# Two transformer blocks in one program: the first product of the feed-forward and of the perceptron is made in turned form, with weights stationary

## What is computed

```python
def swiglu(h, w_ffn_in, w_ffn_out):                 # first block, layers l = 0, 1
    gu = h @ w_ffn_in                               # 256x1024 @ 1024x5632
    g, u = gu[..., :FFN_HIDDEN], gu[..., FFN_HIDDEN:]
    return (jax.nn.silu(g) * u) @ w_ffn_out         # 256x2816 @ 2816x1024

def sq_relu_mlp(x, w_in, w_out):                    # second block, layers i = 0, 1
    return jnp.square(jax.nn.relu(x @ w_in)) @ w_out   # 1024x4096, 4096x1024

for l in range(DEPTH):
    mod = (cond @ ada_w[l] + ada_b[l])[:, None, :]  # 1024x6144 per layer
    ...
    h = rmsnorm(x, norm2_g[l]) * (1 + sc2) + sh2
    x = x + g2 * swiglu(h, w_ffn_in[l], w_ffn_out[l])
```

## Time and profile before

| | us |
|---|---|
| median of 3 runs (1517.55 to 1520.44) | 1519.28 |
| the profiled execution's own time | 1520.99 |
| its span, first to last instruction | 1519.2 |
| PE busy | 1477.3 (97%) |
| POOL busy | 1217.4 (80%) |
| DVE busy | 714.1 (47%) |
| ACT busy | 711.8 (47%) |
| DMA moved | 313.79 MB, 207 GB/s |
| PE's granted clock, mean | 0.993 |

### The profile page before, as it was taken

The page is one execution under the profiler, slowest core; times in us unless marked ns, Lnnn a source line. Parts: engine busy times, 40 slices in busy tenths (PEclk is TensorE's granted clock), DMA queues, the critical chain, the costliest instruction groups (busy, mean ns, idle before and its releaser), DMA issues.

```text
span 1519.2 us, 20262 instructions
## 1 busy us (share of the span) xinstructions
PE 1477.3 (97%) x7242; PEld 1223.3 (81%) x7242; DVE 714.1 (47%) x1398; ACT 711.8 (47%) x1074; POOL 1217.4 (80%) x984
## 2 busy tenths in 40 slices
PE   7999999999999999999999999999999999999997
PEld 4897788788888987888788887878888887788886
DVE  7576755665643758755532104265331043644212
ACT  3335554544444444554544444365554345455432
POOL 4789997698797986548799897907998978289994
PEclk9999999999999999999999999999999999999999
DMA  9995555699876985425676675624665656166553
GB/s 357 323 379 162 183 155 164 203 356 298 288 267 182 385 293 163 132 93 181 208 245 196 192 221 158 211 74 140 193 191 185 208 171 213 45 175 194 185 184 107
DMA packets 168238, 313.79 MB, mean 207 GB/s; under 512 B 11061, under 2 KB 36041, under 8 KB 168137
## 3 DMA queue, kind: packets, MB, share of 16 engines
q1 hardware_dynamic: 166384, 311.15, 63.9%
q10 hardware_dynamic: 1754, 1.35, 0.3%
HBM read 311.39 MB, written 1.06 MB: 206 GB/s over the span
## 4 chain that ended last, share of the span: by engine, by line
PE 82%; POOL 7%; DVE 5%; ACT 2%; DMA 2%; issue 1%; SPq 0%; DVEq 0%; ACTq 0%; POOLq 0%
PE bank L693 72%; POOL lo_units L656 6%; PE bank L2076 2%; PE bank L838 1%; DMA raw_units<-in_w_in 1%; PE bank L859 1%; POOL mod_rows L633 1%; PE bank L827 1%; PE bank L826 1%; PE bank L825 1%; ACT hi_units L1112 1%; PE bank L877 1%; DMA mod_rows<-in_ada_w 1%; DVE bank L1434 1%; POOL mod_rows L637 1%
## 5 line engine op out<-in xcount | busy, mean ns | idle before, releaser
L656 POOL TENSOR_TENSOR lo_units<-raw_units,hi_units 128x512 fp32r<-128x512 f32 (+3 forms) x944 | 1167.7, 1272 | 264.8 <-ACT hi_units L1112 263.6
L693 PE MATMUL bank<-hi_units,turned 128*128 128x512 f32 (+2 forms) x2688 | 834.2, 385 | 7.7 <-POOL lo_units L656 6.0
L1112 ACT ACTIVATE hi_units<-raw_units 128x1024 fp32r<-128x1024 f32 (+3 forms) x478 | 485.5, 1018 | 539.4 <-PE bank L693 433.2
L693 PEld LDWEIGHTS bank<-hi_units,turned 128*128 128x128 f32 x2688 | 502.5, 189 | 103.4 <-POOL lo_units L656 9.0
L693 PE MATMUL bank<-lo_units,turned 128*128 128x512 f32 (+3 forms) x1344 | 512.2, 381 | 0.0
L693 PE MATMUL bank<-hi_units,turned_wide 128*128 128x512 f32 x992 | 312.1, 392 | 1.9 <-DVE turned_wide L1482 1.9
L693 PEld LDWEIGHTS bank<-lo_units,turned 128*128 128x128 f32 x1344 | 254.3, 189 | 41.8 <-issue 0.2
L693 PEld LDWEIGHTS bank<-hi_units,turned_wide 128*128 128x128 f32 x992 | 186.9, 188 | 41.2 <-DVE turned_wide L1482 2.2
L693 PE MATMUL bank<-lo_units,turned_wide 128*128 128x512 f32 x496 | 193.8, 391 | 0.0
L1434 DVE SCALAR_TENSOR_TENSOR bank<-ada_units,small,bank 128x512 f32<-128x512 f32 x144 | 108.8, 756 | 51.9 <-DMA ada_units<-in_ada_w 47.7
L693 PEld LDWEIGHTS bank<-lo_units,turned_wide 128*128 128x128 f32 x496 | 93.6, 189 | 19.2 <-issue 0.2
(11 more groups left out here) (235 smaller groups left out, 1239.2 us busy)
## 6 DMA issues: line engine op xcount, KB each, us to landing
ada_units<-in_ada_w SPq DMA_DIRECT2D x88, 512.0 KB, 7.5
raw_units<-in_w_ffn_in SPq DMA_DIRECT2D x80, 512.0 KB, 4.7
raw_units<-in_mlp_w_in SPq DMA_DIRECT2D x64, 512.0 KB, 3.8
raw_units<-in_mlp_w_out SPq DMA_DIRECT2D x64, 512.0 KB, 3.3
raw_units<-in_w_in SPq DMA_DIRECT2D x56, 458.0 KB, 7.1
raw_units<-in_w_in SPq DMA_DIRECT2D x48, 512.0 KB, 3.9
raw_units<-in_w_ffn_out SPq DMA_DIRECT2D x44, 512.0 KB, 4.4
raw_units<-in_moba_w_qkv SPq DMA_DIRECT2D x24, 512.0 KB, 3.9
```

The lines of the kernel that those rows point to most:

```text
L656: pool.tensor_tensor(LO[:, s, b, 0:w], RAW[:, u["slot"], b, 0:w], HI_[:, s, b, 0:w].bitcast(F32), ALU.subtract).then_inc(lo_ready.sem, lo_ ...
L693: ins = pe.matmul(BANK[2 * c["pair"] + t][:, 0:w], xs[:, part, :], W[:, s, b, 0:w], start=(i == 0 and m == 0 and q == 0), stop=(i == len(c ...
L1112: act.activation(HI_[:, s, 0:n, 0:w], RAW[:, u["slot"], 0:n, 0:w], ACT.Copy)\
```

## The change

The first chunk (512 columns) of gates, of ups and of the perceptron's hidden width stays as it was. All the rest is made in turned form. The weights of one unit are now one 128-column tile of the output over all eight k-tiles, which the host lays out beforehand as 128 rows of 1024 values (`in_tiles`), so a row that SP's queue brings is 4 KB where it was 2 KB. In `turned_unit` the weight tile is the stationary operand; for each k-tile its high half meets `A[:, kt, :, :]`, both halves of the activations side by side as 512 moving columns, and its low half meets the high half of the activations, 256 columns, in the same bank. So the left half of the bank holds two passes, the right half the third, and DVE adds them when it reads (`both_parts`, a reduction over two). The result stands turned, 128 hidden features by 256 tokens, and needs no transpose.

A chunk is now two such tiles: gate and up of one tile (`fft`, 18 for each layer), or two tiles of the perceptron (`mit`, 14 for each layer), each tile in a bank of its own. For `fft`, DVE reduces the gate's bank, ACT takes tanh, DVE reduces the up's bank and multiplies twice (`scalar_tensor_tensor`); for `mit` DVE reduces and squares with ReLU in one instruction. Then ACT copies the high half of the hidden tile into `AT` (`hidden_hi`) and DVE makes the low half (`hidden_lo`), one tile late. `wide` waits for tiles instead of turned chunks.

```diff
@@ program, PE
+        def turned_unit(c, i, A):
+            u = c["units"][i]
+            if i == 0:
+                pair_free(c)
+            s = u["index"] % NH
+            bank = BANK[2 * c["pair"] + i]
+            for kt in range(KT):
+                b, at = divmod(kt * P, CW)
+                if at == 0:
+                    pe.wait_ge(lo_ready.sem, lo_ready.at((u["index"], b)))
+                pe.matmul(bank[:, :], HI_[:, s, b, at:at + P], A[:, kt, :, :].rearrange("p two s -> p (two s)"), start=kt == 0, stop=False)
+                ins = pe.matmul(bank[:, 0:S], LO[:, s, b, at:at + P], A[:, kt, 0, :], start=False, stop=kt == KT - 1)
+            ins.then_inc(unit_used.sem, unit_used.mark(u["index"]))
...
+            for n in range(CW // P, FFN // P):
+                turned_product(("fft", l, n), first_turn if n == CW // P else None)
+                sums()
...
+            for n in range(CW // P, DFF // P, 2):
+                turned_product(("mit", i, n), first_turn if n == CW // P else None)
@@ program, ACT (feed-forward)
+            for n in range(CW // P, FFN // P):
+                prep_chunk(("fft", l, n), NH - 1)
+                if n == CW // P:
+                    turn_hi_ffn(("a", l), 0, CW // P)
+                act.wait_ge(rows.sem, rows.at(("gate tile", l, n)))
+                act.activation(TGN[:, n % 2, 1, :], TGN[:, n % 2, 0, :], ACT.Tanh, scale=0.5)\
+                    .then_inc(act_side.sem, act_side.mark(("tg", l, n)))
+                prep_chunk(("fft", l, n))
+                if n > CW // P:
+                    hidden_hi(("a", l), n - 1, TGN[:, (n - 1) % 2, 3, :])
@@ program, DVE
+        def hidden_lo(tag, n, h):
+            dve.wait_ge(turned_hi.sem, turned_hi.at((tag, "hidden", n)))
+            tell(v.tensor_tensor(AT[:, n, 1, :], h, AT[:, n, 0, :].bitcast(F32), ALU.subtract), turned_lo, (tag, "tile", n))
+        def both_parts(out, bank):
+            return v.tensor_reduce(out, bank[:, :].rearrange("p (two s) -> p s two", two=2), AX_X, ALU.add)
...
+            for n in range(CW // P, FFN // P):
+                key = ("fft", l, n)
+                g, tg, u, h = (TGN[:, n % 2, m, :] for m in range(4))
+                say(both_parts(g, tile_product(dve, key, 0)), ("gate tile", l, n))
+                if n == CW // P:
+                    turn_lo_ffn(("a", l), 0, CW // P)
+                else:
+                    hidden_lo(("a", l), n - 1, TGN[:, (n - 1) % 2, 3, :])
+                if n < FFN // P - 1:
+                    before(key)
+                tell(both_parts(u, tile_product(dve, key, 1)), drained, key)
+                dve.wait_ge(act_side.sem, act_side.at(("tg", l, n)))
+                link(v.scalar_tensor_tensor(tg, tg, 1.0, g, ALU.add, ALU.mult))
+                say(v.scalar_tensor_tensor(h, tg, 0.5, u, ALU.mult, ALU.mult), (("a", l), "hidden", n))
+                after(key)
...
+            for n in range(CW // P, DFF // P, 2):
+                key = ("mit", i, n)
+                for m in (n, n + 1):
+                    s, h = RTN[:, 2 * (m % 4), :], RTN[:, 2 * (m % 4) + 1, :]
+                    ins = both_parts(s, tile_product(dve, key, m - n))
+                    ...
+                    say(v.scalar_tensor_tensor(h, s, 0.0, s, ALU.max, ALU.mult), (("a2", i), "hidden", m))
+                    ...
+                        hidden_lo(("a2", i), m - 1, RTN[:, 2 * ((m - 1) % 4) + 1, :])
```

More of the change, by code:

```diff
@@ L163, in chunk, with tile_chunk @@
         return c
+    def tile_chunk(key, tiles):
+        c = dict(key=key, kind="gemm", pair=pair[0] % 2, ncols=CW, units=[])
+        pair[0] += 1
+        for name, l, n in tiles:
+            c["units"].append(dict(kind="w", index=count["w"], n=UNIT_K, ncols=CW, src=("tiles", name, l, n)))
+            count["w"] += 1
+        chunks.append(c)
+        return c
     def vec(name, src, col0, ncols=CW):
@@ L201, in phase @@
         made = {}
-        total = sum(-(-args[3] // UNIT_K) for _, args in parts) - lead - tail
+        total = sum(2 if args[0][0] == "fft" else -(-args[3] // UNIT_K) for _, args in parts) - lead - tail
         seen = sent = 0
@@ L1925, in _ @@
-            turn_lo_ffn(("a", l), n_ff - 1, (FFN - (n_ff - 1) * CW) // P)
+            kg, ku = ("ffg", l, 0), ("ffu", l, 0)
+            before(kg)
+            banks = product_ready(dve, kg)
+            dve.wait_ge(act_side.sem, act_side.at(("tg", l, 0)))
+            for t in range(NT):
+                ins = v.scalar_tensor_tensor(TG[:, 0, t, :], TG[:, 0, t, :], 1.0, banks[t][:, :], ALU.add, ALU.mult)
+            tell(ins, drained, kg)
+            after(kg)
+            before(ku)
+            banks = product_ready(dve, ku)
@@ L2101, in traced, with in_tiles @@
     return nc
+def in_tiles(inputs):
+    out = {}
+    for name, to in (("w_ffn_in", "w_ffn_tiles"), ("mlp_w_in_2", "mlp_w_tiles_2")):
+        w = np.asarray(inputs[name])
+        tiles = w.reshape(w.shape[0], KT, P, -1, P).transpose(0, 3, 2, 1, 4)
+        out[f"in_{to}"] = np.ascontiguousarray(tiles).reshape(w.shape[0], -1, P, D)
+    return out
 def kernel(**inputs):
```

173 lines of the change are left out of this document (79 added, 94 removed).

## The result

The changed kernel takes 1630.12 us (median of 4 runs, 1628.43 to 1638.27) where the kernel before takes 1519.86 beside it (4 runs): a ratio of 1.0739, with a 95% interval of 1.0716 to 1.0762. That is +110 us where +76 was forecast.

The account below looks back on a forecast made before the run. DVE's round in the feed-forward was to replace PE as the bound: layer 0 +49.5, layer 1 +21.7, SP's queue +8, perceptrons -3, together +76 on 1519.3, so 1595 us; range 1542 to 1632.

Parts of the forecast that it names:

- the upper sum: Whole kernel: large waits for POOL, 20 us for the queue and 11 for the clock give 1630 us.
- large waits for POOL: Feed-forward chunk: DVE's three waits for POOL at the upper end of 0.37 to 0.82 us, making a round 7.0 us.
- weight loads not covered: Rival: where wide and narrow matmuls alternate, 69 ns for each narrow one, +31 us in the perceptron, 1626 us; chance 0.04.
- PE's matmuls and the weight loads: Turned loops: wide-narrow pairs take 0.347 us with loads covered, +1.3 us each feed-forward, +1.5 each perceptron.
- the forecast of -4.6 without the stall: Each perceptron, PE alone: matmuls +1.5 us and seven turns gone -6.1, leaving out the 3.1 us stall.
- DVE's round of 6.6 us: Feed-forward chunk: reductions 1.38, ACT 1.85, three DVE instructions 1.27, POOL waits 2.1 us, against PE's 5.55; layer 1 +21.7.
- The modulation adds in full: Feed-forward: modulation lies in DVE's same order, so it adds all 47.2 us in layer 0 and 13.2 in layer 1.
- SP's queue in layer 0, +8: Layer 0's feed-forward: weight units issued late behind ada units cost 1.5 us in six of 18 rounds, nothing to 20.
- Nothing for the stretch behind layer 0: From layer 0's second product to layer 1's loop: no difference forecast, 0 us.
- The perceptron, -3: Both perceptrons: only PE's sum counts, 2 x (1.5 - 6.1 + 3.1), -3 us.
- the stall: Each perceptron: the remaining turn waits for ACT's ReLUs and DVE's squarings, so PE stalls about 3.1 us.
- Clock, nothing in the sum: PE's clock after idle time: no term in the sum, up to 11 us above it in the range.

Follow-up runs that it names:

- mlp_late_bank: Feed-forward of the kernel before, perceptron turned, its first chunk's transposes one tile later and its hidden tile in a free bank: 1510.10 us, ratio 0.9942.
- mod_short: Changed kernel, but six of eight instructions adding up each modulation chunk in the feed-forwards work on 64 of 512 columns (incomplete modulation): 1614.90 us, ratio 1.0629.
- less_ahead: Changed kernel, but in the feed-forward ACT makes high halves of one unit fewer before tanh and the hidden tile's copy: 1598.71 us, ratio 1.0521.
- all_five: all_four, and in the feed-forward's last chunk DVE also takes modulation standing in SP's stream among the second product's first units: 1512.13 us, ratio 0.9953.
- hi_early: Changed kernel, but ACT copies the previous hidden tile's high half before the next gate tile and the next units' high halves: 1548.31 us, ratio 1.0189.
- early_first: hi_early, and DVE's modulation comes ahead of the low half of the hidden tile before: 1548.48 us, ratio 1.0179.
- all_four: early_first with no_lock's free banks, and in the perceptron the first chunk's transposes one tile later: 1516.06 us, ratio 0.9978.
- no_lock: Changed kernel, but reduced gate and up tiles and hidden tiles stand in free banks, not SBUF (first turned tile excepted): 1594.10 us, ratio 1.0471.
- ffn_only: Changed kernel with the perceptron of the kernel before, so only the feed-forward is turned: 1631.98 us, ratio 1.0734.
- mlp_late: Feed-forward of the kernel before, perceptron turned, its first chunk's transposes one tile later: 1511.07 us, ratio 0.9948.
- mlp_only: Changed kernel with the feed-forward of the kernel before, so only the perceptron is turned: 1521.87 us, ratio 1.001.

## Why the prediction was off

The sign, the bound (DVE's round in the feed-forward) and most of layer 1 came as forecast; the time was 35 us short. That the upper sum was also 1630 is luck: it was made of large waits for POOL, 20 us of queue and 11 of clock, and what was measured is 29 us of queue, 16 behind the loop, and of clock only some 3, in the perceptrons. The rival that came out at the same time, weight loads not covered, is not what happened. Step by step:

- **PE's matmuls and the weight loads: right.** A pair of a wide and a narrow matmul starts every 0.347 us in the perceptrons of `mlp_late_bank`, the number that was forecast. The Trainium skill (TensorE: Matmul & The Clock Gate, "The mechanism") has weight loads overlap matmuls in flight only where the row group differs. The trace doesn't agree: each of these matmuls has a load of its own over all 128 rows, with a record of 188 ns (median), and two matmuls with two such loads fit into 0.347 us, so the loads run beside the matmuls. With the turns gone, 77.7 us against 81.1 is -3.4 in a perceptron's window; the forecast of -4.6 without the stall is -3.7 there, since one turn of 0.87 stood behind it.
- **DVE's round of 6.6 us: right.** In layer 1 the reductions take 0.69, the waits for POOL 2.15 a round (forecast 2.1), and DVE's idle time before the low half 1.8. 17 rounds from 849.4 to 978.3 us are 7.58 each; forecast were 6.6 and 0.73 of modulation. Over the loop this is the +26.0 against +21.7.
- **The modulation adds in full: right for layer 0**, by `mod_short` (15.4 of 16.3 us); in layer 1 it gave back 1.8 of 4.2.
- **SP's queue in layer 0, +8: this is the step that failed.** By `less_ahead` it was 29 us in the loop. The prediction saw the slot's wait and SP's single stream, but priced it as a late unit of 1.5 us in six rounds, on the ground that ACT is up to six units ahead. It is a ring: DVE's lateness keeps the queue late, each lap takes a landing of some 5 us, and DVE's idle time before the low half, 3.5 us a round, was 1.7 more than ACT's hop.
- **Nothing for the stretch behind layer 0: wrong, +16.** The prediction gave no reason for it; this is the second step that failed. Around 3 us of it are this execution's. Opening the ring and the locks brings it from 349.5 to 342.5, the queue at the end of the loop (`all_five`) another 4. The remaining 5 stay open.
- **PE's wait at the modulation's sum: left out.** 21.1 and 5.7 us of PE's idle time stand there. It is no term of its own, since it comes from the same lateness of DVE: it is gone in `all_five`'s loops with the rest.
- **The perceptron, -3: the stall was right (2.9 us for 3.1), the clock and a slower pitch behind it were left out.** The changed kernel lost 4.4 us in the two loops and got back 1.6 in the stretches behind them, +2.8 in all. In each perceptron 1.5 us are the pitch of 0.353 in place of 0.347, and 1.2 to 1.5 the clock. That locks don't bind there was right.
- **Clock, nothing in the sum: right for layer 0.** Its granted clock was 0.84, but DVE's reductions waited only 1.5 us for PE in the whole loop, so a faster PE would have stood longer. With the idle time gone (`hi_early`) the clock is 0.99 without being touched. The up to 11 us that the range added for it are shown by no run; in the perceptrons, where PE is the bound, the clock cost 1.2 to 1.5 us each.

## What to carry to other kernels

When an instruction of one engine waits for another engine, list what stands ahead of the releaser in its program, and ask of each item whether a queue that waits for the first engine feeds it: a ring like that has a full transfer in each lap, and no engine looks busy in it. Two changes of order, each of one step, were worth 82 and 58 us here, each more than the locks (36 us) and than all of PE's savings. They don't add up: both together gave 82. The views that show a ring are the queue's own waits and DMA's share of the chain, not busy shares.

## What was not expected of the hardware

A DVE instruction with two inputs in SBUF doesn't always wait for only one of POOL's. POOL in the changed kernel, then DVE at the same time:

```profile
533.54 26.05 POOL L674 TENSOR_TENSOR lo_units<-raw_units,hi_units 128x512 fp32r<-128x512 f32 x21
```

```profile
538.28 22.46 DVE L1556 TENSOR_TENSOR bank<-x_rows,mod_rows 128x512 f32<-128x512 f32 x2
```

POOL ran 21 instructions of 1.24 us without a pause, and of DVE's two, the first took 21.86 us and ended just after POOL paused at 559.6; in `hi_early` the same one took 0.86. It is no accident of one execution: `early_first`, `all_four`, `no_lock`, `mod_short`, `ffn_only` and `all_five` have one of 20.5 to 21.9 us too. Here PE's other work covered it but for about 1 us: PE waited 1.3 us behind it for the rows that follow, 0.2 in `hi_early`. The Trainium skill (SBUF — State Buffer, "SBUF: two separate sides") says of a DVE instruction with two SBUF inputs and a GpSimd instruction that the one that starts first has the shared ports for the whole of it. The waits of the loops, 0.55 to 0.83 us on average, agree; one instruction's worth would have been 1.24 us here, and 21.86 is not explained by it. Why DVE gets its turn in some series of POOL's and not in others was not tried.

PE's pace has a second, small step at a granted clock of 1.00. Narrow matmuls start 0.347 us apart in the first perceptron of `mlp_late` and 0.353 in the second, and 0.353 in both of `mlp_only` and of the changed kernel, evenly in every part of the loops that was timed. That is 1.5 us a perceptron. The cause is open.
